# First z slot merged with the decay inputs ahead of the mixer's rounds, and round eight with two weight slots instead of three

## What is computed

```python
h = rms_norm_2(x, g_mix[i])
proj = h @ w_in[i]
glu_a, glu_b, q, k, v, z, a_in, b_in, gate_a, gate_b = split_cols(proj, IN_SIZES)
...
g = -jnp.exp(a_log[i]) * jax.nn.softplus(a_in + dt_bias[i])
beta = jax.nn.sigmoid(b_in)
o_fwd = gated_delta_rule(q, k, v, g[:, :, 0], beta[:, :, 0])
...
o = rms_norm_2(o_fwd + o_bwd, delta_norm_g[i]) * jax.nn.silu(z)
```

## Time and profile before

| | us |
|---|---|
| median of 3 runs | 1201.29 (1198.54 to 1202.06) |
| profiled execution | 1202.13 |
| its span | 1200.3 |
| TensorE busy | 1171.7 (98%) |
| VectorE busy | 839.7 (70%) |
| ScalarE busy | 701.5 (58%) |
| GpSimd busy | 324.8 (27%) |

### The profile page before, as it was taken

The page is one execution under the profiler, slowest core; times in us unless marked ns, Lnnn a source line. Parts: engine busy times, 40 slices in busy tenths (PEclk is TensorE's granted clock), DMA queues, the critical chain, the costliest instruction groups (busy, mean ns, idle before and its releaser), DMA issues.

```text
span 1200.3 us, 21345 instructions
## 1 busy us (share of the span) xinstructions
PE 1171.7 (98%) x8592; PEld 1088.5 (91%) x8592; DVE 839.7 (70%) x1519; ACT 701.5 (58%) x1181; POOL 324.8 (27%) x257
## 2 busy tenths in 40 slices
PE   8999999999999999999999999999999999999997
PEld 7777899998887799998899999999989989999886
DVE  6796588884685578885558787889954656555456
ACT  5466576663467676664466667667666445444344
POOL 1172300000028300000156666675555220000010
PEclk9999999999999999999979999999999999999999
DMA  7633355546553366555333332332223646555542
GB/s 286 252 141 141 125 210 210 184 181 216 176 178 139 124 244 211 202 188 211 141 137 118 132 111 104 140 109 102 105 72 108 226 176 222 209 186 201 203 154 81
DMA packets 31587, 199.74 MB, mean 166 GB/s; under 512 B 4289, under 2 KB 6481, under 8 KB 8706
## 3 DMA queue, kind: packets, MB, share of 16 engines
q1 hardware_dynamic: 29506, 189.27, 44.1%
q0 software_dynamic: 1840, 8.60, 1.9%
q10 hardware_dynamic: 144, 0.52, 0.1%
HBM read 197.33 MB, written 1.05 MB: 165 GB/s over the span
## 4 chain that ended last, share of the span: by engine, by line
PE 85%; DVE 7%; ACT 3%; issue 2%; POOL 1%; DMA 1%; SPq 0%; POOLq 0%; ACTq 0%; DVEq 0%
PE ps L1190 24%; PE ps L1192 23%; PE ps L1191 23%; PE ps L1567 2%; PE ps L1583 1%; PE ps L1344 1%; PE ps L1363 1%; DVE conv L2773 1%; PE ps L1331 1%; DVE wlo L2387 1%; PE ps L1215 1%; DVE ps L2842 1%; PE ps L1284 1%; PE ps L1197 1%; DVE x L2516 1%
## 5 line engine op out<-in xcount | busy, mean ns | idle before, releaser
L1190 PE MATMUL ps<-halves,whi 128*128 128x256 f32 x1472 | 410.7, 279 | 0.1
L1191 PE MATMUL ps<-halves,whi 128*128 128x256 f32 x1472 | 405.7, 276 | 0.0
L1192 PE MATMUL ps<-halves,wlo 128*128 128x256 f32 x1472 | 405.6, 276 | 0.0
L2387 DVE TENSOR_TENSOR wlo<-raw,whi 128x2048 fp32r<-128x2048 f32 (+1 forms) x133 | 300.7, 2263 | 116.1 <-ACT whi L1847 112.9
L1847 ACT ACTIVATE whi<-raw 128x2048 fp32r<-128x2048 f32 (+1 forms) x143 | 269.3, 1885 | 95.6 <-PE ps L1192 91.4
L1190 PEld LDWEIGHTS ps<-halves,whi 128*128 128x128 f32 x1472 | 283.3, 192 | 0.8 <-DVE halves L2981 0.5
L1192 PEld LDWEIGHTS ps<-halves,wlo 128*128 128x128 f32 x1472 | 283.4, 193 | 0.0
L1191 PEld LDWEIGHTS ps<-halves,whi 128*128 128x128 f32 x1472 | 283.4, 193 | 0.1
L1114 POOL TENSOR_TENSOR wlo<-raw,whi 128x1024 fp32r<-128x1024 f32 x72 | 172.4, 2404 | 54.5 <-ACT whi L1856 53.9
L1006 POOL TENSOR_TENSOR rstd<-sumsq,half_power 128x1 f32<-128x1 f32 x14 | 11.5, 823 | 573.9 <-ACT xn L1874 406.4
L1190 PE MATMUL ps<-whi,halves 128*128 128x512 f32 (+4 forms) x440 | 149.1, 339 | 3.6 <-DVE halves L2490 2.7
(11 more groups left out here) (337 smaller groups left out, 1849.3 us busy)
## 6 DMA issues: line engine op xcount, KB each, us to landing
raw<-in_stream SPq DMA_DIRECT2D x176, 1024.0 KB, 4.8
gain<-in_gains POOLq DMA_DIRECT2D x7, 512.0 KB, 5.6
bias<-in_rel POOLq DMA_DIRECT2D x1, 1536.0 KB, 8.5
raw<-in_stream SPq DMA_DIRECT2D x2, 648.0 KB, 7.9
cst<-in_consts POOLq DMA_DIRECT2D x1, 1280.5 KB, 8.9
raw<-in_stream SPq DMA_DIRECT2D x2, 528.0 KB, 4.2
x<-in_x SPq DMA_DIRECT2D x2, 512.0 KB, 4.6
out<-xn SPq DMA_DIRECT2D x4, 256.0 KB, 2.4
```

What stands on the lines that cost most here:

```text
L1190: nc.tensor.matmul(out, a_hi, b_hi, start=start, stop=False)
L1191: nc.tensor.matmul(out, a_hi, b_lo, start=False, stop=False)
L1192: return nc.tensor.matmul(out, a_lo, b_hi, start=False, stop=stop)
L2387: dve.tensor_tensor(used(wlo, n), used(raw, n), used(whi, n).bitcast(F32), ALU.subtract)\
```

## The change

The narrow slot "ab" and the first z slot are replaced by two "columns" slots, ("z_decay", 0) and ("z_decay", 1), which hold 288 columns (z heads 0 and 1, and the 32 decay inputs) for the upper and the lower half of the 1024 rows. Their products, 24 matmuls of 288 columns per tile, stand where `ab_products` stood and go to banks 4 and 5. VectorE writes the remainders of the first half, GpSimd those of the second. The number of slots ahead of round 0 is now two, so that q,k 0 is `last + 3` and v 0 is `last + 4`. In the rounds the other slots move up; rounds 0 to 7 keep their number of slots, and round 8 has two.

```diff
-    plan.append(("narrow", "ab", ("w_in_2", 0), 6144, 32))
+    rows_major("z_decay", ("w_in_2", 0), [(5120, 2 * P), (6144, 32)])
...
-    other = [glu[0:2], [z[0]] + glu[2:4], [glu[4], z[1]], [z[2], glu[5], z[3]], [glu[6], gates[0]],
-             [glu[7]] + gates[1:2], gates[2:3], gates[3:5]]
+    other = [glu[0:2], glu[2:4] + [z[1]], [glu[4], z[2]], [glu[5], z[3], gates[0]], [glu[6], gates[1]],
+             [glu[7]] + gates[2:3], gates[3:4], gates[4:6]]
...
-    return made + [gates[5:8], out]
+    return made + [gates[6:8], out]
...
-        POOL_SLOTS = [slot_of[key] + AHEAD for key, r, tick in MIX_SLOTS if 0 <= r < len(ROUNDS)]
+        POOL_SLOTS = [slot_of[key] + AHEAD for key, r, tick in MIX_SLOTS if 0 <= r < len(ROUNDS)] + [slot_of[("z_decay", 1)]]
```

GpSimd, between and behind the norm's two tiles, and TensorE:

```diff
                 if t == 0:
-                    split_shared(("qk", 0))
+                    n = slot_of[("z_decay", 1)]
+                    pool.wait_ge(*S["weights_high"].at((n, 1)))
+                    pool.tensor_tensor(used(wlo, n), used(raw, n), used(whi, n).bitcast(F32), ALU.subtract)\
+                        .then_inc(*S["pool_weights_low"].one((n, 1)))
 
             pool.memset(sum_row[:, :].bitcast(F32), 0.0).then_inc(*S["rows_cleared"].one("mixer"))
             pool.memset(glu_in[:, :, :], 0.0).then_inc(*S["glu_cleared"].one())
+            split_shared(("qk", 0))
...
+            def first_z_and_decay_products(t):
+
+                for half in range(2):
+                    n = slot_of[("z_decay", half)]
+                    if t == 0:
+                        wait_low(pe, n)
+                    wait_split(5, t, (half,))
+                    wh, wl = used(whi, n), used(wlo, n)
+                    for i in range(4):
+                        kt = 4 * half + i
+                        last = three(ps[:, 4 + t, 0:Z_DECAY], xhi[:, kt, t * P:(t + 1) * P], xlo[:, kt, t * P:(t + 1) * P],
+                                     in_order(wh[:, i, :]), in_order(wl[:, i, :]), kt == 0, kt == KT - 1)
+                    if t:
+                        last.then_inc(*S["weights_used"].one(n))
...
                 pe.wait_ge(*S["inverse_begun"].at(h))
+                if h == 0:
+                    pe.wait_ge(*S["tanh_used"].at(("z", 0)))
```

ScalarE casts one slot more behind the norm (`split(last + 4)`), and the second half of slot glu 0 is cast in tick 2 of round 0, not in tick 1 behind the decay logs. VectorE's `norm_behind_down` splits z_decay's first half (`split(last + 2)`) before the norm of tile 0, and its half of q,k 0 (`split(last + 3)`) behind the last remainders of the norm. The first z slot is read from banks 4 and 5 in tick 7 of round 0:

```diff
+            def first_z():
+
+                act.wait_ge(*S["weights_used"].at(slot_of[("z_decay", 1)]))
+                act.wait_ge(*tanh_free(TANH_BEFORE[("z", 0)]))
+                act.activation(tanh[:, TANH_OF[("z", 0)], :].rearrange("p (t c) -> p t c", t=2), ps[:, 4:6, 0:2 * P], ACT.Tanh,
+                               scale=0.5).then_inc(*S["tanh_made"].one(("z", 0)))
...
+                    if (r, i) == (0, 2):
+                        split_half(slot_of[slot_at(0, 1)] + AHEAD, 1)
-                    if slot_at(r, i):
+                    if slot_at(r, i) and (r, i) != (0, 1):
                         split_half(slot_of[slot_at(r, i)] + AHEAD, i % 2)
...
+            def first_z():
+
+                dve.wait_ge(*S["tanh_made"].at(("z", 0)))
+                dve.scalar_tensor_tensor(xn[:, :, 0:TOK], tanh[:, TANH_OF[("z", 0)], :].rearrange("p (t c) -> p t c", t=2), 1.0,
+                                         ps[:, 4:6, 0:2 * P], ALU.add, ALU.mult).then_inc(*S["tanh_used"].one(("z", 0)))
...
-                link(dve.tensor_copy(ab[:, 0, :, :], ps[:, 3, 0:64].rearrange("p (t c) -> p t c", t=2)))
+                link(dve.tensor_copy(ab[:, 0, :, :], ps[:, 4:6, 2 * P:Z_DECAY]))
```

More of the change, by code:

```diff
@@ L175, in pack_stream @@
                 out[n].reshape(P, KT, 2 * P)[:] = evens_first(out[n].reshape(P, KT, 2 * P))
-        elif kind == "narrow":
-            a, c = args
-            out[n].reshape(P, KT, 256)[:, :, 0:c] = w[:, a:a + c].reshape(KT, P, c).transpose(1, 0, 2)
         elif kind == "down":
@@ L547 @@
 AB_SPINS = (6, 2)
+Z_DECAY = 2 * P + 32
 END_SPINS = (5, 8)
@@ L556 @@
 NORMS = len(GAINS) - 1
-MIX_SLOTS = [("ab", -1, 0)] + [(slot[0], r, 2 * i) for r, slots in enumerate(ROUNDS) for i, slot in enumerate(slots)] \
+MIX_SLOTS = [(("z", 0), -1, 0)] + [(slot[0], r, 2 * i) for r, slots in enumerate(ROUNDS) for i, slot in enumerate(slots)] \
     + [(("delta_out", i), len(ROUNDS), 0) for i in range(KT // 2)]
@@ L585, in finished_slot @@
     return slot_at(r, i - 1) if i else slot_at(r - 1, TICKS - 1)
+FIRST_Z_AT = (0, 7)
 def tanh_order():
@@ L595, in tanh_order @@
                 order.append(key)
+            if (r, i) == FIRST_Z_AT:
+                order.append(("z", 0))
             if r < HEADS and i == 3:
@@ L825, in weights_of @@
                 return at.rearrange("p (k c) -> p k c", k=4)[:, :, 0:sum(c for _, c in entry[3])]
-            if entry[0] == "narrow":
-                return at.rearrange("p (k c) -> p k c", k=KT)[:, :, 0:entry[4]]
             return at
@@ L1452, in half_slot @@
                     last.then_inc(*S["weights_used"].one(n))
[L1454 to L1465, removed]
-                    last.then_inc(*S["weights_used"].one(n))
+            def first_z_and_decay_products(t):
[11 more added lines that the diff above has]
+                        last.then_inc(*S["weights_used"].one(n))
             def decay_sums():
@@ L1777, in _ @@
                 turn_norm(5, t)
-                ab_products(t)
+                first_z_and_decay_products(t)
                 if t == 0:
@@ L1914, in norm_behind_down @@
                 round_turned(5 if k == 4 else k, [(1, 0), (1, 1)])
+                if k == 4:
+                    split(last + 4)
             def split_first(n, half):
@@ L2301, in _ @@
                         evacuate(finished_slot(r, i))
+                    if (r, i) == FIRST_Z_AT:
+                        first_z()
                     if r < HEADS and i == 3:
@@ L2456, in norm_behind_down @@
                     scale_x(0)
+                    split(last + 2)
                 normalize(after, [0])
@@ L2470, in norm_behind_down @@
                 lows(after, [(1, 0), (1, 1)])
+                if k == 4:
+                    split(last + 3)
             def split_first(n, half):
@@ L2718, in decay_inputs @@
             def decay_inputs():
-                dve.wait_ge(*S["weights_used"].at(slot_of["ab"]))
+                dve.wait_ge(*S["weights_used"].at(slot_of[("z_decay", 1)]))
                 dve.wait_ge(params2_loaded, 16)
-                link(dve.tensor_copy(ab[:, 0, :, :], ps[:, 3, 0:64].rearrange("p (t c) -> p t c", t=2)))
+                link(dve.tensor_copy(ab[:, 0, :, :], ps[:, 4:6, 2 * P:Z_DECAY]))
                 dt = row_at["dt_bias_2"].unsqueeze(1).broadcast_to([P, TT, 16])
@@ L3032, in _ @@
             decay_inputs()
-            split(slot_of["ab"] + AHEAD)
+            split(slot_of[("z_decay", 1)] + AHEAD)
             for r in range(len(ROUNDS)):
```

## The result

The changed kernel takes **1210.22 us** (median of 4 runs, 1209.21 to 1211.16) against 1201.50 for the kernel before on the same chip: ratio 1.0073, 95% interval 1.0054 to 1.0092, so slower by 0.7%. The forecast was 1197.3 with 1194.0 to 1201.0, so it has the wrong sign and misses by 13 us. The profiled execution took 1210.29 us (span 1208.4), close to the median.

What follows compares the result with a forecast made beforehand. TensorE, busy for 98% of the span, was taken to bound the kernel. Entry terms of -4.7 us and +0.7 in round eight summed to -4.0, so 1197.3 us against the median of 1201.29, range 1194.0 to 1201.0.

Steps and rivals of the forecast that it cites:

- Cost nothing: Entry: GpSimd's remainder of z_decay's second half is ready near 596.7, ahead of its use at 598.8; 0 us.
- 288 columns: Entry: the merged products of 288 columns take about 0.122 us each at full clock.
- Tile 1 at full clock: Entry: the clock stays at 2.4 GHz, so tile 1's products gain -2.2 us and its transposes -0.5.
- First slot at full clock and decay logs: Entry: first slot's products at full speed, -1.8 us; decay logs delay ScalarE's q,k 0 copy, +0.5.
- GpSimd freed: Entry, tile 1's norm: GpSimd's small step is faster once VectorE's split moves behind the norm; -0.7 us.
- The order of the slots: Rounds one to seven keep their slots, taps and waits; zero, between -0.5 and +1.0 us.
- Round 8: One slot less, but the clock falls in 905 to 908.4 and is back about 911; +0.7 us.
- rival A: Full clock in round eight as well: -1.25 us there, -6.0 in all, 1195.3 us; chance 0.18.
- C: Entry clock falls anyway between the two tiles' products, and round eight gives +3.4: slower, 1206.4 us; chance 0.07.
- B: Round eight's end spins run slow throughout (+3.4), or the rounds lose as much in VectorE's queue: 1200.0 us; chance 0.17.
- D: Entry: 288 columns do not run at 0.122, or tile 1 waits for GpSimd's half: 1199.5 us; chance 0.05.

Runs made afterwards that it cites:

- d: The changed kernel with 8 filling matmuls ahead of step five and of step six of round 8: 1207.34 us, ratio 1.0051.
- b1: The changed kernel with ScalarE casting half 1 of the first glu slot at tick 1 of round 0 again: 1207.97 us, ratio 1.0054.
- b2: The changed kernel with GpSimd's half of tick 2 in round 0 waiting for VectorE's gates of q,k 0: 1203.96 us, ratio 1.0028.
- g_gate_spins: The changed kernel with GpSimd waiting for norm and q,k 0 gates, round 8 filling matmuls, and 5 more ahead of q,k 0's turn: 1196.51 us, ratio 0.9967.
- f: The changed kernel with GpSimd waiting for tile 0's norm and q,k 0's gates, and filling matmuls ahead of round 8's steps five and six: 1199.21 us.
- e2: The kernel before with a GpSimd memset of 2,048 columns added behind the deviation of tile 0: 1201.19 us (one run).
- a1: The changed kernel with GpSimd's remainder of z_decay's half 1 waiting for VectorE's norm of tile 0: 1207.11 us, ratio 1.0044.
- a2: The changed kernel with GpSimd's 1,152-column remainder cut into four instructions of 288 columns: 1206.12 us, ratio 1.0045.
- c: The changed kernel with GpSimd waiting both for tile 0's norm and for the gates of q,k 0: 1201.26 us, ratio 1.0003.

## Why the prediction was wrong

**The wrong step** is the one on GpSimd's remainder of z_decay's second half, "Cost nothing". I asked whether the remainder is ready in time for TensorE (it was) and not what it does to VectorE, which runs its norm at that moment. It cost 2.0 us by the lock, and 2.25 by the fall of the clock behind the new wait, which two of the four traces with this wait in the changed order have (after and d, not b1 and b2). The hint stood in the earlier trace rows: the small GpSimd step took 0.97 us beside VectorE's split of two SBUF inputs against 0.27 without it. I read that as something GpSimd suffers and booked its end as a gain, and did not turn it round.

**The step that is missing** is the cast that moves from tick 1 to tick 2. The prediction priced what it does on ScalarE's queue but not the third half that it puts on GpSimd's pile just ahead of the gates: 3.7 us in stage C, and, as TensorE stood for 4.8 us, 3.65 us more of slow clock in D (13.16 against 9.51); all four traces with this wait have that fall. A moved step counts on every queue behind it.

The rest, term by term:

- *288 columns*: the products of tile 1 start 0.122 us apart (608.36 to 611.05 over 22 distances, behind a first distance of 0.23), forecast 0.122. Right.
- *Tile 1 at full clock*, forecast -2.2 - 0.5 = -2.7: stage B is -2.61. Right.
- *First slot at full clock and decay logs*, forecast -1.8 + 0.5 = -1.3: stage C with the lock away (g_gate_spins) is -1.23. Right, though hidden in the changed kernel under the 3.7.
- *GpSimd freed*, forecast -0.7: the small step is 0.27 us again, but stage A without the lock gives -0.44. Mis-sized by 0.26: the step takes 0.70 less but begins 0.24 later behind the turn of tile 0 (5.54 us in g_gate_spins against 5.30).
- *The order of the slots*, forecast 0 (-0.5 to +1.0): stage E is +0.30, all of it in round 0 and 1; the distance then stays at 7.37 us within 0.02 for rounds two to seven. In stage D, b2 and g, where the clock holds, still have +0.37 over before; its cause stays open.
- *Round 8*, forecast +0.7: F is +0.74. The mechanism was right, the closeness in part luck: in the other kernels without spins F is +0.45 to +1.53, by where the fall begins. Against the shift of 7.37, step five would be at 903.84 (forecast 903.8), step six at 906.96 (907.0), and the clock falls at 904.5 and is back at 911.3 (forecast back about 911). The timeline of TensorE after, in round 8:

```profile
911.21 0.66 PE L1575 MATMUL ps<-prod,inv_t 128*128 128x128 f32 x4 [2.25 <-DVE prod L2913]
911.71 0.87 PE L1597 MATMUL ps<-inv_t,prod 128*128 128x128 f32 x4
914.33 1.11 PE L1580 MATMUL ps<-prod,inv_t 128*128 128x128 f32 x4 [1.74 <-DVE prod L2913]
```

With the clock kept up, rival A's term for this round was -1.25, and F in d, f and g is -1.38.

With the locks away, the change does what the forecast said of stages B and C, of A but for 0.26 us, and, without filling products there, of F. That g's 1196.51 is near the forecast of 1197.3 is no confirmation of the sum, as g has spins that the change does not have and that bring 3.3 us; with the two waits alone the median is 1201.26. As made, the one term that was written as nothing and the one that was left out weigh 11.6 us together in these traces (2.0 + 2.25 + 3.7 + 3.65).

One more weakness was in the baseline. The forecast took its clock terms at the entry from one trace, with a fall of 13.7 us. The fastest runs of the kernel before have a mean clock of 0.996, which is about 10 us at the 1.2 GHz level in all (an estimate: 0.004 of 1197 us, doubled). So they can't have had that fall in full, and for them those terms were smaller.

**The rivals.** C had the right side and half the mechanism ("the clock falls at the entry all the same"), but put the fall between the two tiles' products; it came ahead of the first ones, and the first slot ran at full clock. A fell: the clock did fall in round 8. Its evidence was one execution: the clock stayed up behind the 2.1 us wait at 110.76 there, but fell 0.2 to 1.3 us behind that wait in four of the kernels here. B's price has an error in its sum: 912.25 + (16 + 18) x 0.11 is 916.0, so +2.5 and not +3.4, and C uses the same +3.4. Neither B's slow end spins nor D's dearer product is in the trace: F is +0.74 and the products are 0.122 apart.

Of the falls in the changed kernel each begins in a wait of TensorE or within 1 us behind one (2.0, 4.8 and 2.25 us), and g_gate_spins, which has the same wide products and no wait over 1.2 us at these places, has none. The Trainium skill, page "TensorE: Matmul & The Clock Gate", section "What's actually happening", ties the fall to idleness; these traces agree, and waits of this length were enough in some executions and not in others. Idleness is not all of it, though. In the kernel before and in e2 the clock fell (600.74 and 599.84) more than 3 us behind the last wait, which was of 1.2 us, while TensorE was busy with 32-column products and spins; a1, a2, c, f and g have the same wait of 1.2 us, 288 columns behind it, and no fall there. That is what the forecast had expected of the wider product, but no run here separates the columns from chance.

## What to carry to other kernels

When a step is given to GpSimd, or moved in its queue, look at what VectorE runs at that moment: if it has two inputs in SBUF, whoever is second waits for the whole instruction of the first. Put a wait on GpSimd behind VectorE's short urgent instructions, or cut GpSimd's piece; either is cheap as long as GpSimd has slack (27% busy here). And where a weight slot is taken out of a stretch that waits on other engines, keep TensorE at work in the waits that it leaves: 21 filling products were worth 3.3 us here (2.1 in round 8, 1.2 at the turn), and in the changed kernel's trace each lock cost its own time again in slow clock behind it.

## What the runs showed that I had not expected

- The lock's price is set by the piece, not by the amount of work: 3.98 us of GpSimd in four pieces held VectorE 0.55 us, 3.09 us in one piece held it 2.4.
- VectorE's instructions with an input in PSUM are not held: the 96 taps of the short convolutions in the kernel before take 470 to 484 ns each, beside a remainder of GpSimd (618.99, with GpSimd at work to 622.36) as without one (683.52, GpSimd idle).
- The clock's falls differ between executions. All twelve traces have the same wait of 2.1 us near 110 us in the first block, whose code is the same in all. In a1, b1, c and f the clock falls behind it, in the other eight it does not; from that wait to the turn of tile 0 is 485.9 to 486.0 us in the first group and 484.3 to 484.4 in the second, so the fall costs 1.6 us. (Up to 1.3 us of difference between traces is older than that wait.) One trace shows only one draw.
- Counted over the twelve traces: behind the wait of 2.0 us at the norm with 288 columns a fall in two of four, behind 2.25 us in round 8 in six of six, behind 4.8 us at the turn of q,k 0 in four of four, behind 2.0 us there (b1) in one of one, and behind 1.07 us there in two of three (c and f, not b2).
- A fall once begun lasted 3.4 us at the least and 13.7 at the most in these traces (but for the one that the end cuts off), so a wait of 1.1 us (c_both) cost 1.2 us again behind it.
